# Spreading rows of a decoder trunk from four partition groups instead of one, with the decay sums spread after the last z projection

## What is computed

```
h = RMSNorm(x); z = h @ w_in
A: gated DeltaNet, 4 heads      B: latent attention, 8 heads      C: mLSTM, 4 heads
x += w_out( sum_b sigmoid(gate_b) * (o_b @ w_branch_b) )
x += ConvFFN(RMSNorm(x))
```

```
G = jnp.cumsum(g, axis=-1)
dec_incl = jnp.exp(jnp.where(incl, G[..., :, None] - G[..., None, :], -jnp.inf))
A = beta[..., :, None] * einsum('bnhld,bnhmd->bnhlm', k, k) * jnp.where(strict, dec_incl, 0.0)
QK = einsum('bnhld,bnhmd->bnhlm', q, k) * dec_incl
q_dec = q * jnp.exp(G)[..., None]
```

## Time and profile before

| | us |
|---|---|
| median of 3 runs (lowest, highest) | 1474.86 (1474.51, 1476.02) |
| the profiled execution | 1478.7 |
| its span, first to last instruction | 1476.9 |
| PE busy | 1379.1 (93%) |
| DVE busy | 491.4 (33%) |
| ACT busy | 273.5 (19%) |
| POOL busy | 178.4 (12%) |
| mean granted clock of PE | 0.973 of 2.4 GHz |
| line L515, the weight products | 1058.4 of PE's busy time |

### The profile page before, as it was taken

One profiled execution on the slowest core, in us unless ns is written; L12 is line 12 of the kernel. 1 busy time (PEld: TensorE's weight loads), 2 busy tenths in 40 slices (PEclk: granted clock), 3 DMA queues, 4 the chain that ended last, 5 costly groups with the idle time before them and its releaser, 6 DMA issues.

```text
span 1476.9 us, 18904 instructions
## 1 busy us (share of the span) xinstructions
PE 1379.1 (93%) x7716; PEld 1140.3 (77%) x7716; DVE 491.4 (33%) x1163; ACT 273.5 (19%) x646; POOL 178.4 (12%) x230
## 2 busy tenths in 40 slices
PE   3999989999999899989989999899999979999894
PEld 3878967777887788878768799677688868888783
DVE  2764255422121333320048434562211223333101
ACT  1331132422100111100014212243220011111000
POOL 1014234120000000000100241442000000000000
PEclk9989999999999999999989899999999999999997
DMA  6422237441343244444444223564224424444320
GB/s 247 143 91 72 86 94 260 162 185 58 121 151 133 100 148 152 142 134 142 140 152 136 69 72 93 194 214 173 99 81 147 137 97 142 152 148 144 133 100 30
DMA packets 58278, 194.82 MB, mean 132 GB/s; under 512 B 7440, under 2 KB 7504, under 8 KB 55120
## 3 DMA queue, kind: packets, MB, share of 16 engines
q1 hardware_dynamic: 49248, 149.97, 30.4%
q0 software_dynamic: 8944, 43.64, 8.5%
HBM read 184.32 MB, written 9.25 MB: 131 GB/s over the span
## 4 chain that ended last, share of the span: by engine, by line
PE 92%; DVE 3%; ACT 2%; issue 1%; DMA 1%; POOL 0%; DVEq 0%; ACTq 0%; POOLq 0%
PE banks L515 70%; PE banks L956 2%; PE banks L634 1%; PE banks L555 1%; PE banks L649 1%; PE banks L962 1%; PE banks L583 1%; PE banks L862 1%; PE banks L1006 1%; PE banks L965 1%; DVE arena L1436 1%; DMA arena<-in_x 1%; PE banks L623 1%; PE banks L950 1%; PE banks L657 1%
## 5 line engine op out<-in xcount | busy, mean ns | idle before, releaser
L515 PE MATMUL banks<-arena 128*128 128x264 f32 x4576 | 1058.4, 391 | 33.8 <-DVE arena L1436 22.8
L515 PEld LDWEIGHTS banks<-arena 128*128 128x128 f32 x4576 | 870.6, 192 | 199.5 <-DVE arena L1436 24.5
L1083 ACT ACTIVATE arena<-banks 128x512 f32<-128x512 f32 (+6 forms) x296 | 119.8, 432 | 524.4 <-PE banks L515 338.9
L1926 DVE TENSOR_SCALAR arena<-arena 128x256 f32<-128x256 f32 x44 | 18.2, 414 | 157.6 <-ACT arena L1083 157.6
L2127 POOL COPY arena<-arena 128x2 f32<-128x2 f32 x44 | 14.0, 317 | 406.3 <-ACT arena L1083 406.3
L1955 DVE SCALAR_TENSOR_TENSOR arena<-banks,arena 128x264 f32<-128x264 f32 x16 | 6.9, 433 | 155.0 <-PE banks L515 155.0
L555 PE MATMUL banks<-arena 128*128 128x264 f32 x64 | 20.6, 490 | 24.3 <-ACT arena L1119 19.3
L2028 POOL TENSOR_TENSOR arena<-arena 128x512 f32<-128x512 f32 x28 | 30.8, 1120 | 84.5 <-PE banks L634 47.3
L555 PEld LDWEIGHTS banks<-arena 128*128 128x128 f32 x64 | 15.5, 249 | 29.0 <-issue 19.7
L1114 ACT ACTIVATE arena<-banks 128x264 f32<-128x264 f32 x32 | 12.6, 392 | 129.4 <-PE banks L515 129.4
L1616 DVE TENSOR_TENSOR arena<-arena,banks 128x512 f32<-128x512 f32 x24 | 16.4, 689 | 55.2 <-PE banks L649 52.6
(11 more groups left out here) (402 smaller groups left out, 1188.5 us busy)
## 6 DMA issues: line engine op xcount, KB each, us to landing
arena<-in_weights SPq DMA_DIRECT2D x230, 512.0 KB, 3.2
arena<-in_weights SPq DMA_DIRECT2D x112, 256.0 KB, 3.1
arena<-in_s POOLq DMA_DIRECT2D x2, 2048.0 KB, 13.0
out_ss_o<-arena POOLq DMA_DIRECT2D x16, 256.0 KB, 3.2
arena<-in_mla_w POOLq DMA_DIRECT2D x4, 1024.0 KB, 8.2
arena<-in_c POOLq DMA_DIRECT2D x4, 512.0 KB, 6.0
out_sc_o<-arena POOLq DMA_DIRECT2D x16, 128.0 KB, 2.7
arena<-in_x POOLq DMA_DIRECT2D x1, 1056.0 KB, 11.2
```

What stands on the lines that cost most here:

```text
L515: mm = nc.tensor.matmul(dst, ring[:, at_:at_ + 128], rhs[:, j, :], start=(start and j == 0), stop=(stop and j == k - 1))
L1083: return A(dst, src, ACT.Copy, scale=scale)
L1926: link(ts(cv, fc[:, j % 3, 0:TP], w[0], par[:, Q_FB + j:Q_FB + j + 1], ALU.mult, ALU.add))
```

## The change

1. After the rows are complete, ACT issues three DMAs that copy the first five of the ten rows (4 partitions by 1320 numbers, 21 KB each) to partitions 32 to 35, 64 to 67 and 96 to 99. The rows are renumbered so that the five that are spread stand first. A new signal, rows_copied, counts the landings.
2. A spread of head h reads its four rows and its selector from partitions 32 h to 32 h + 3.
3. In PE's list pz 3 comes before bcG; before bcG, PE waits for the three copies. ACT takes Exp of `dec` after the tanh of pz 3, and DVE gates pz 3 before the eight subtractions.

The banks are dealt by the list, so pz 3 now gets bank 2, bcG 0 to 3 banks 3 to 6, and the first output of the two weight banks, pm 0, follows bcG 3 in bank 6, where it followed pz 3.

```diff
-    add("pz", 3, "V"); add("rowT", 1, "V"); add("bcG", 4, "V"); add("pz", 1, "V", 3)
+    add("pz", 3, "V"); add("rowT", 1, "V"); add("pz", 1, "V", 3); add("bcG", 4, "V")
...
-        rows = fix.take3(10, TT)[0:4]
-        R_G, R_B, R_EG, R_KD, R_BEG, R_W, R_M, R_INT, R_EMR, R_WK = range(10)
+        row_groups = fix.take3(10, TT)
+        rows = row_groups[0:4]
+        R_G, R_B, R_EG, R_M, R_INT, R_KD, R_BEG, R_W, R_EMR, R_WK = range(10)
...
                     b = claim(name, h)
-                    nc.tensor.matmul(b[:, 0:last - first], ident[0:4, h:h + 1].to_broadcast((4, P)), rows[:, row, first:last],
-                                     start=True, stop=True).then_inc(out_ready, 1)
-
+                    s = 32 * h
+                    nc.tensor.matmul(b[:, 0:last - first], ident[s:s + 4, s + h:s + h + 1].to_broadcast((4, P)),
+                                     row_groups[s:s + 4, row, first:last], start=True, stop=True).then_inc(out_ready, 1)
+
+                project("pz", 3, hn)
+                pe.wait_ge(*at(l, "rows_copied", 48))
                 for h in range(NH):
                     spread("bcG", h, R_G, 0, TP)
-                project("pz", 3, hn)
...
                 A(l2sq[:, :, TP:TT], qkv[:, 0:8, TP:TT], ACT.Square).then_inc(*up("qk_squares"))
+                act.wait_ge(*at(l, "rows_dve", 1))
+                for s in (32, 64, 96):
+                    nc.scalar.dma_start(row_groups[s:s + 4, 0:R_INT + 1, :], rows[:, 0:R_INT + 1, :]).then_inc(*up("rows_copied", 16))
                 for j in range(4):
-                    if j == 3:
-                        act.wait_ge(*evac(l, "bcG", 3))
-                        A(dec, dec, ACT.Exp).then_inc(*up("decay_exp"))
                     act.wait_ge(*out(l, "pz", j))
                     A(z[:, j, :], bank("pz", j)[:, 0:TT], ACT.Tanh, scale=0.5).then_inc(*up("z_tanh"))
+                act.wait_ge(*evac(l, "bcG", 3))
+                A(dec, dec, ACT.Exp).then_inc(*up("decay_exp"))
...
+                for j in range(3):
+                    gated(j)
+                dve.wait_ge(*out(l, "rowT"))
+                V.tensor_copy(cols, bank("rowT")[:, 0:48]).then_inc(*read("rowT"))
+                gated(3)
+                dve.wait_ge(*evac(l, "rowT"))
+                for h in range(NH):
+                    b = bank("bcG", h)
+                    dve.wait_ge(*out(l, "bcG", h))
+                    ts(dec[:, h, :], b[:, 0:P], cols[:, h:h + 1], 0.0, ALU.subtract, ALU.min)
+                    ts(dec[:, 4 + h, :], b[:, P:TP], cols[:, 24 + h:25 + h], 0.0, ALU.subtract, ALU.min).then_inc(*read("bcG", h))
```

More of the change, by code:

```diff
@@ L207 @@
     l2_root=1, na_root=1, query_blocks=1, row_e=1, row_ea=1,
-    row_ln=1, row_m=1, row_m0=1, row_u=1, row_x=1, rows_act=1, rows_dve=1, s_decayed=8, s_loaded=16,
+    row_ln=1, row_m=1, row_m0=1, row_u=1, row_x=1, rows_act=1, rows_copied=48, rows_dve=1, s_decayed=8, s_loaded=16,
     sample_pads=1, window_zero=1, sconv=1, sconv_tanh=1, silu=13, squares=2, st_ckv=16, st_conv=16, st_ffn=16,
@@ L1530, in _, with gated @@
                 stt(qkv[:, 0:12, TP:TT], ths, 1.0, cvs, ALU.add, ALU.mult).then_inc(*up("silu"))
[L1531 to L1540, removed]
+                def gated(j):
                     dve.wait_ge(*at(l, "z_tanh", j + 1))
                     stt(z[:, j, :], z[:, j, :], 1.0, bank("pz", j)[:, 0:TT], ALU.add, ALU.mult).then_inc(*read("pz", j))
+                for j in range(3):
[9 more added lines that the diff above has]
+                    ts(dec[:, 4 + h, :], b[:, P:TP], cols[:, 24 + h:25 + h], 0.0, ALU.subtract, ALU.min).then_inc(*read("bcG", h))
                 dve.wait_ge(*evac(l, "l2"))
```

## The result

| | median, us | lowest to highest | runs |
|---|---|---|---|
| kernel before, on the same chip | 1475.75 | 1473.48 to 1478.42 | 10 |
| changed kernel | 1480.08 | 1478.19 to 1485.54 | 10 |

The ratio is 1.0035, with a 95% interval of 1.002 to 1.005: slower, by some 5 us. The prediction said 1473.9, at most 1478.0, and gave "slower" a chance of 0.18.

A forecast was written before the change was run, and what follows sets the result against it. PE, 92% of the chain that ended last, was taken as the bound. Gains of 0.92 and 2 x 0.02 us took the profiled 1478.7 to 1477.7; the median, 3.8 lower, gave 1473.9, range 1470.2 to 1478.0.

The forecast's parts named there:

- pz 3 at full clock behind rowT: In each layer pz 3 follows rowT at once and takes 3.75 us at full clock, instead of 5.20.
- The sum of the move, 0.46 us to bcL: With bcG behind pz 3, the first bcL spread starts at 99.68 instead of 100.14, 0.46 us earlier.
- The copies, landing in 2.2 to 3.2 us: ACT's copies before bcG land 2.2 to 3.2 us after issue, by 91.75, so PE does not wait.
- The rival: Copies land late and PE stands before bcG: at 7.2 us to landing, +5.9 us, 1480.7; chance 0.18.
- bcE, 0.23 us per pair: Packed bcE spreads save 0.23 us per pair where PE never idles; two pairs, two layers: 0.92 us.
- bcB, bcM and bcI, no gain: Packing these spreads shortens PE's own time but gains 0, since DVE's reads of the banks set the pace.
- The clock at 0.50 when bcL begins: PE idles before bcL, so its clock is at half there; 0.44 us lost, leaving 0.02 us per layer.
- The sum: Gains of 0.92 us from bcE and 2 x 0.02 from the move: 0.96 us, giving 1473.9.
- a rival in which a fall disappears: Earlier work prevents a clock fall after a wait on DVE, saving 1.7 us per layer: 1470.5; chance 0.18.

The follow-up runs named there:

- e1: Kernel before with the new order alone: pz 3 ahead of bcG, no copies, every spread from partitions 0 to 3; 1479.59 us, ratio 1.0031.
- e3: Changed kernel with the three copies issued right behind ACT's last row, some 10 us sooner; 1485.87 us, ratio 1.0076.
- e4: Changed kernel with bcG unpacked, read from partitions 0 to 3, and the wait for the copies moved before bcB; 1480.4 us, ratio 1.0052.

## Why the prediction was wrong

- *pz 3 at full clock behind rowT*: right, 3.83 us against 3.75.
- *The sum of the move, 0.46 us to bcL*: right in e1, e3 and e4 (0.5 to 0.6 us). In the changed kernel the late copies took it and more.
- *The copies, landing in 2.2 to 3.2 us*: wrong, 4.07, with issues of 0.58 to 1.18 us each instead of 0.33. The rival was right in kind: break-even was put at 3.8 us, and at 4.07 its own sum loses 0.26 us per layer; layer 1 lost 0.9, since the slower issues also put the last copy 0.55 us later behind rowT than I had. But it gives only 1.1 us in all up to bcL, and e1, which has no copies, loses 3.9 us all the same. So this rival does not explain the result, and "slower" with its chance of 0.18 came true for another reason than the one given.
- *bcE, 0.23 us per pair*: right, 0.22.
- *bcB, bcM and bcI, no gain*: right; PE waits for DVE's reads.
- *The clock at 0.50 when bcL begins*: wrong for the traced layers. In layer 1 the clock had fallen at 95.68 already and was back when bcL began at 100.48; in layer 2 it fell at 819.30, 0.57 us after bcL had begun.

```profile
95.81:99.22 3.41, 3.41 (x8) 2.38 (x8) 0.60 (x1) 2.75 (x3) 2.00 (x1) 0.52 0.32 107
99.22:102.63 3.41, 2.25 (x18) 1.52 (x18) 2.61 (x5) 0.00 (x0) 0.00 (x0) 0.98 0.14 52
```

- *The step that failed* is "The sum": it added local terms and took the rest of the program as unchanged. The clock falls at the large waits, and how long it stays low depends on where within a few tenths of a microsecond PE starts again. Behind n2 that was worth 2.7 us in the changed kernel's trace and 2.5 to 3.0 us per layer in e1 to e4, where the sum had nothing; the medians moved by 4.3 us the other way. The kernel before happened to stand on the cheap side of that behind n2, in both layers: that is luck of position. I had named this only as a rival in which a fall disappears, that is, as a gain; the same mechanism with the other sign was left out, and it decided. From the trace of before one could have seen it: its clock table, of which the earlier trace rows has a few stretches, has a fall at each of the four waits of 5.7 us, and behind n2 PE started 0.59 and 0.52 us after it, for 3.4 us at half clock. At n1 of layer 2 PE started 0.67 us after a fall (734.64), half clock lasted 6.8 us, and the norm sums took 6.84 us, where those of n2 took 3.84. So the room behind n2 was 0.1 to 0.15 us:

```profile
735.31 6.84 PE L555 MATMUL banks<-arena 128*128 128x264 f32 x16 [2.69 <-ACT arena L1119]
```

- The range ended at 1478.0 for the same reason: two layers with one more 3.4 us at half clock behind n2 and behind fd are 5.4 us (2.7 each), which should have stood in it. Its upper end was also not what it said: by the rival's own sum copies of 5 us give 1476.3, and 1478.0 belongs to 5.8 us.

Open: what the executions without a trace did. There is one trace of each kernel. The changed kernel's is of its fastest execution and has the loss in layer 2 alone; that of before is 3.8 us above its median. How the three executions at 0.965 and those of e3 at 0.966 come about is not shown. For the thought that packed bcM and bcI make a fall at sk more likely the traces give nothing: sk is slow in 8 of 20 places with packing and in 11 of 16 without.

## What to carry to other kernels

Where PE's clock falls at long waits, a change of a few tenths of a microsecond anywhere ahead of a wait can cost or give back several microseconds behind it, so a tuned kernel's time is partly luck of position. Fill PE's known waits with idle matmuls in a free bank before comparing variants of such a kernel; here that was worth 1.1%, more than any of the reorderings, and it made the variants alike within 0.2%. And read the mean granted clock of every timed run beside its time: one trace can be of the luckiest execution.

## What the runs showed that I had not expected

- A copy of 4 partitions by 1320 numbers inside SBUF, issued by ACT, lands 4.07 us after its issue, later than 512 KB of weights from HBM (3.2 us); three issues in a row hold ACT for 2.41 us.
- One extra matmul of 0.44 us per layer costs 5.2 us, and four cost about as much.
- Half clock on PE can cost DVE or be free: a multiply that came 2.3 us later met POOL's long one and took 5.71 us instead of 3.06; in 17 other places it came later, met neither, and took 1.44 to 1.67.
